# Second block of a two-block model: in-projections in the order head, unit, side work in a fixed 128-point period, and an out projection split in two

## The reference

```python
proj = jnp.einsum('btd,dc->btc', h, w_in[l].astype(jnp.float32))
rw = _token_shift(proj[..., :RWKV_COLS], shift_mu[l])
hg = proj[..., RWKV_COLS:]
...
o_rwkv, v_first = _rwkv7_branch(rw, v_first, ...)
o_hgrn = _hgrn2_branch(hg, lower_bounds[l], g_norm_w[l])
y = jnp.einsum('btc,cd->btd', jnp.concatenate([o_rwkv, o_hgrn], axis=-1), w_out[l])
h = _layer_norm(ALPHA * h + y, ln_w[l], ln_b[l])
```

## Time and profile before

| what | us |
|---|---|
| median of 3 runs | 3117.43 |
| lowest, highest | 3116.45, 3124.18 |
| span of the profiled execution | 3114.6 |
| PE busy | 3019.7 (97%) |
| DVE busy | 1697.0 (54%) |
| ACT busy | 1213.4 (39%) |
| POOL busy | 283.4 (9%) |

### The profile page before, as it was taken

How to read it: one execution, slowest core, us unless ns; L and a number is a source line. 1 busy time by engine, 2 the same in 40 slices (tenths; PEclk the granted TensorE clock), 3 DMA queues, 4 the chain that set the end, 5 groups by cost and what they waited for, 6 DMA issues and landing times.

```text
span 3114.6 us, 39362 instructions
## 1 busy us (share of the span) xinstructions
PE 3019.7 (97%) x15418; PEld 2423.6 (78%) x15418; DVE 1697.0 (54%) x2880; ACT 1213.4 (39%) x2131; POOL 283.4 (9%) x517
## 2 busy tenths in 40 slices
PE   9999999999999999999999999999999999999897
PEld 7778787878788877777778868787787887868786
DVE  6554545454543336556553364656666666565647
ACT  5443434343433324434343333434444343434422
POOL 0110101010100000000000002202022020212001
PEclk9999999999999999999999999999999999999999
DMA  4222222222243321221233322212222131224334
GB/s 164 82 77 84 78 82 82 82 82 82 82 135 131 106 88 62 68 75 62 68 122 134 122 85 80 83 55 90 75 70 90 61 97 56 89 72 140 135 129 155
DMA packets 86007, 288.99 MB, mean 93 GB/s; under 512 B 12080, under 2 KB 12720, under 8 KB 85568
## 3 DMA queue, kind: packets, MB, share of 16 engines
q1 hardware_dynamic: 69696, 243.66, 23.9%
q0 software_dynamic: 16128, 42.81, 4.5%
HBM read 261.13 MB, written 25.17 MB: 92 GB/s over the span
## 4 chain that ended last, share of the span: by engine, by line
PE 83%; DVE 9%; ACT 4%; issue 2%; DMA 1%; POOL 1%; DVEq 0%; ACTq 0%; SPq 0%; POOLq 0%
PE bank L280 14%; PE bank L282 14%; PE bank L281 14%; PE bank L284 7%; PE bank L286 7%; PE bank L285 7%; PE bank L1370 2%; PE bank L1301 1%; PE bank L1306 1%; DVE mc_split L736 1%; PE bank L337 1%; PE bank L317 1%; ACT mc_split L568 1%; PE bank L472 1%; PE bank L485 1%
## 5 line engine op out<-in xcount | busy, mean ns | idle before, releaser
L280 PE MATMUL bank<-ma_split,mc_split 128*128 128x512 f32 x2304 | 957.1, 415 | 12.7 <-DVE ma_split L890 7.7
L736 DVE TENSOR_TENSOR mc_split<-mc,mc_split 128x1024 fp32r<-128x1024 f32 x434 | 534.9, 1233 | 790.1 <-ACT mc_split L568 789.0
L282 PE MATMUL bank<-ma_split,mc_split 128*128 128x512 f32 x2304 | 905.8, 393 | 0.0
L281 PE MATMUL bank<-ma_split,mc_split 128*128 128x512 f32 x2304 | 902.4, 392 | 0.0
L568 ACT ACTIVATE mc_split<-mc 128x1024 fp32r<-128x1024 f32 x434 | 457.8, 1056 | 658.5 <-PE bank L284 349.6
L280 PEld LDWEIGHTS bank<-ma_split,mc_split 128*128 128x128 f32 x2304 | 436.8, 190 | 121.5 <-issue 49.1
L282 PEld LDWEIGHTS bank<-ma_split,mc_split 128*128 128x128 f32 x2304 | 434.6, 189 | 97.0
L281 PEld LDWEIGHTS bank<-ma_split,mc_split 128*128 128x128 f32 x2304 | 436.9, 190 | 78.7 <-issue 4.4
L284 PE MATMUL bank<-mc_split,ma_split 128*128 128x512 f32 x576 | 230.2, 400 | 5.0 <-DVE mb L1780 3.4
L286 PE MATMUL bank<-mc_split,ma_split 128*128 128x512 f32 x576 | 225.3, 391 | 0.0
L285 PE MATMUL bank<-mc_split,ma_split 128*128 128x512 f32 x576 | 224.7, 390 | 0.0
(11 more groups left out here) (366 smaller groups left out, 3732.6 us busy)
## 6 DMA issues: line engine op xcount, KB each, us to landing
mc<-in_w SPq DMA_DIRECT2D x434, 512.0 KB, 3.5
x<-mc POOLq DMA_DIRECT2D x8, 1024.0 KB, 5.2
y<-mb_split SPq DMA_DIRECT2D x28, 256.0 KB, 2.5
ma_split<-y POOLq DMA_DIRECT2D x28, 256.0 KB, 4.5
mb<-in_xt SPq DMA_DIRECT2D x8, 512.0 KB, 9.5
mc<-in_x POOLq DMA_DIRECT2D x4, 1024.0 KB, 5.7
mc<-x POOLq DMA_DIRECT2D x4, 1024.0 KB, 6.5
mats<-mc POOLq DMA_DIRECT2D x32, 128.0 KB, 2.2
```

What stands on the lines that cost most here:

```text
L280: mm = pe.matmul(banks[j][:], wh[:, c], act_hi[:, kt, :], start=(kt == 0), stop=False)
L281: pe.matmul(banks[j][:], wl[:, c], act_hi[:, kt, :], start=False, stop=False)
L282: last = pe.matmul(banks[j][:], wh[:, c], act_lo[:, kt, :], start=False, stop=(kt == KT - 1))
L736: dve.tensor_tensor(w_low[:, s % NR, :, :], w_raw[:, s % NR, :, :], w_high[:, s % NH, :, :].bitcast(F32), ALU.subtract).then_inc(w_lo, 1)
```

## The change

1. **Order of blocks.** rw0, wa, hg0, then rw i, hg i for i = 1 to 7, and then the out blocks. The weights are laid out in the same order.
2. **Period.** All steps of unit u >= 1 begin at 128u+10 (k<12 at two points a step; k 12 to 15 at 2.5; k 16 on at +82, k 25 on at +106, k 36 on at +134). Unit 0 begins at 7 as before. Head h begins at 128h+67 and takes 4.2 points a step (head 7 takes 4.0).
3. **Out blocks.** `most`: kt 0 to 13 of out block 0, 56 points; DVE adds its banks to the residual (`most_take`). Then out block 1, whose last two kt now wait for unit 7 and head 7; then `rest`: kt 14 and 15 of out block 0, 8 points; then out blocks 2 and 3. SP's, POOL's, ACT's and DVE's loops follow the slots; POOL's order of inverses and y loads is as before. Residual loads for group 2 wait for `rest`.

```diff
-BLOCKS = OUT2 + GROUPS
-SLOT0 = [8 * b if b <= WA else 8 * b - 6 for b in range(BLOCKS)]
+OUT2_REST = OUT2 + 2
+BLOCKS = OUT2 + GROUPS + 1
+def slots(b):
+    return {WA: 2, OUT2: BLOCK_SLOTS - 1, OUT2_REST: 1, BLOCKS - 1: 2 * BLOCK_SLOTS}.get(b, BLOCK_SLOTS)
...
-            KIND = [("rw", 0), ("wa", 0), ("rw", 1)]
-            for i in range(UNITS - 2):
-                KIND += [("hg", i), ("rw", i + 2)]
-            KIND += [("hg", i) for i in (UNITS - 2, UNITS - 1)] + [("out", n) for n in range(GROUPS)]
+            KIND = [("rw", 0), ("wa", 0), ("hg", 0)]
+            for i in range(1, UNITS):
+                KIND += [("rw", i), ("hg", i)]
+            KIND += [("most", 0), ("out", 1), ("rest", 0), ("out", 2), ("out", 3)]
...
                 i = k - CHUNKS
-                late = 0 if u else 5
-                if k < PART_B:
-                    return (128 * u - 54 if u else 7) + 2 * k
+                first = 128 * u + (10 if u else 7)
                 if k < CHUNKS:
-                    return 120 * u + 16 + late + 2 * (k - PART_B)
-                begin = 120 * u + 26 + late
+                    return first + 2 * k
+                begin = first + 2 * CHUNKS + 2
                 if i < 4:
-                    return begin + 2 * i
+                    return begin + 5 * i // 2
                 if i < 13:
-                    return begin + 54 + 5 * (i - 4) // 2
+                    return begin + 56 + 5 * (i - 4) // 2
                 if i < CHUNK_K:
-                    return begin + 77 + 5 * (i - 13) // 2
-                return begin + 105 + 3 * (i - CHUNK_K)
+                    return begin + 80 + 5 * (i - 13) // 2
+                return begin + 108 + 3 * (i - CHUNK_K)
...
-                rate = {UNITS - 2: 23, UNITS - 1: 20}.get(h, 45)
-                return 64 * (BLOCK_OF["hg", h] + 1 - LANE0) + 1 + m * rate // 10
+                rate = 40 if h == UNITS - 1 else 42
+                return point0(BLOCK_OF["hg", h] + 1) + 3 + m * rate // 10
...
                         if b == OUT2:
-                            if kt < KT - 2:
-                                pe.wait_ge(y_in[kt // 2], 64)
-                            else:
-                                pe.wait_ge(y_rw_lo if kt == KT - 2 else y_h_lo, UNITS)
+                            pe.wait_ge(y_in[kt // 2], 64)
+                        if b == OUT2 + 1 and kt >= KT - 2:
+                            pe.wait_ge(y_rw_lo if kt == KT - 2 else y_h_lo, UNITS)
...
+            def most_take(dve, b):
+                for t in range(TT):
+                    dve.wait_ge(x2_ready, t + 1)
+                    dve.wait_ge(gemm_done, done(b, t))
+                    dve.tensor_tensor(xr[0][:, t, :], banks[t][:], xr[0][:, t, :], ALU.add).then_inc(bank_free[t], 1)
```

More of the change, by code:

```diff
@@ L56 @@
 OUT2 = RW0 + 2 * UNITS + 1
-BLOCKS = OUT2 + GROUPS
-SLOT0 = [8 * b if b <= WA else 8 * b - 6 for b in range(BLOCKS)]
-TOTAL_SLOTS = SLOT0[-1] + 2 * BLOCK_SLOTS
+OUT2_REST = OUT2 + 2
+BLOCKS = OUT2 + GROUPS + 1
+def slots(b):
+    return {WA: 2, OUT2: BLOCK_SLOTS - 1, OUT2_REST: 1, BLOCKS - 1: 2 * BLOCK_SLOTS}.get(b, BLOCK_SLOTS)
+SLOT0 = [sum(slots(x) for x in range(b)) for b in range(BLOCKS)]
+TOTAL_SLOTS = sum(slots(b) for b in range(BLOCKS))
 Y_ORDER = [*range(UNITS - 1), *range(UNITS, 2 * UNITS - 1), UNITS - 1, 2 * UNITS - 1]
@@ L261, in swa_steps, with products @@
                 return [k for k in range(18) if swa_step_at(g, k) - 8 * s in points]
-            def products(pe, b, lhs_w, act_hi, act_lo, needs, slot0=None, tiles=range(4)):
-                for kt in range(KT):
-                    s = (SLOT0[b] if slot0 is None else slot0) + kt // 2
+            def products(pe, b, lhs_w, act_hi, act_lo, needs, slot0=None, tiles=range(4), kts=range(KT)):
+                first, end = kts[0], kts[-1]
+                for kt in kts:
+                    s = (SLOT0[b] if slot0 is None else slot0) + (kt - first) // 2
                     if kt % 2 == 0:
@@ L1154, in lane_steps @@
                 for point in points:
-                    rw, hg = AT.get(64 * (b - LANE0) + point, ((), ())) if b >= LANE0 else ((), ())
+                    inside = b >= LANE0 and point < 8 * slots(b)
+                    rw, hg = AT.get(point0(b) + point, ((), ())) if inside else ((), ())
                     yield from (("rw", u, k) for u, k in rw)
@@ L1429, in second_pe @@
                         continue
-                    for point in products(pe, b, kind != "out", h_hi, h_lo, needs):
+                    kts = {"most": range(KT - 2), "rest": range(KT - 2, KT)}.get(kind, range(KT))
+                    for point in products(pe, b, kind in ("rw", "hg"), h_hi, h_lo, needs, kts=kts):
                         if b == RW0 and point % 8 == 3:
@@ L1577, in second_act @@
                         continue
-                    for s in range(BLOCK_SLOTS * (1 + (b == BLOCKS - 1))):
+                    for s in range(slots(b)):
                         for lane, u, k in lane_steps(b, range(8 * s, 8 * s + 4)) if s < BLOCK_SLOTS else ():
@@ L1908, in second_dve @@
                             rw_dve(dve, st, u, k) if lane == "rw" else hg_dve(dve, st, u, k)
-                        if kind == "out" and s == 5:
+                        if kind in ("most", "out") and s == 5:
                             dve.wait_ge(x2_in[n % 2], 32 * (n // 2 + 1))
@@ L1917, in second_dve @@
                         hg_take(dve, st, n, b)
+                    elif kind == "most":
+                        most_take(dve, b)
                     elif b < BLOCKS - 1:
@@ L2038, in second_pool @@
                     if n >= 2:
+                        taken = OUT2_REST if n == 2 else OUT2 + 1
                         for t in range(TT):
-                            pool.wait_ge(bank_free[t], freed(OUT2 + n - 1, t))
+                            pool.wait_ge(bank_free[t], freed(taken + 1, t))
                     pool.dma_start(xr[n % 2], x2_rows[:, :, n * N:(n + 1) * N]).then_inc(x2_in[n % 2], 16)
@@ L2131 @@
     wa = w2[:, lo:hi].reshape(2, 8, P, P).transpose(0, 2, 1, 3).reshape(2, P, 2 * N)
-    parts = [w1, rw[0], wa, rw[1]]
-    for i in range(UNITS - 2):
-        parts += [hg[i], rw[i + 2]]
-    parts += [hg[UNITS - 2], hg[UNITS - 1], blocks(x["w_out_2"][0].reshape(KT, P, D)[Y_ORDER].reshape(D, D))]
-    parts.append(parts[-1][-BLOCK_SLOTS:])
+    parts = [w1, rw[0], wa, hg[0]]
+    for i in range(1, UNITS):
+        parts += [rw[i], hg[i]]
+    last = blocks(x["w_out_2"][0].reshape(KT, P, D)[Y_ORDER].reshape(D, D)).reshape(GROUPS, BLOCK_SLOTS, P, 2 * N)
+    parts += [last[0, :-1], last[1], last[0, -1:], last[2], last[3], last[3]]
     w1 = np.concatenate(parts)
```

20 lines of the change are left out of this document (12 added, 8 removed).

## The result

The changed kernel takes 3178.2 us in the median (3175.2 to 3179.1), the kernel before 3117.0 in the same comparison: ratio 1.0189, 95% interval 1.0176 to 1.0202. It is 1.9% slower. The forecast was 3169, with a range from 3132 to 3200. The profiled executions are 3173.4 and 3114.6 us long, 58.8 apart, where the sum had said 51.

A forecast was written before the change was run, and what follows sets the result against it. PE, busy 97% of the span, was taken as the bound, so only its idle time and clock could change. New losses 126.1 us less old 75 gave +51 on 3114.6: 3166 profiled, 3169 us median, range 3132 to 3200.

The forecast's parts named there:

- unit 0's 7.4: Unit 0 keeps its N wait of 4.3, 0.9 at the block's start and its clock, with small additions: 7.4 us.
- Part 1, the squeezed end goes: Heads 6 and 7 get more points a step; 13.9 us at L1370 and the rest of the old 75 us go.
- Part 2, the collision: New unit's first steps meet old unit's end and a head's steps on DVE: PE waits 7.4 us a unit, most at B.
- The prediction's own sign: In the changed kernel's profile, waits under 2 us at B (step 10) would mean the DVE sum is wrong.
- The take: DVE's `rw_take` starts late by 0.9 and k=32's copy stands behind it: together 1.9 us a unit.
- the shared bank: k=0 and m=17 at one point use one bank, so PE waits 0.7 us; the second place counted in the 7.4.
- Part 2, the clock: Slow PE clock after waits: 2.0 us a unit and 3.0 after the stall, against 20 lost in the old pattern.
- Part 3, POOL's queue: The y loads behind unit 7's inverse leave PE idle 26.1 us at the first matmul of `most`; bounds 24 and 32.
- The rival without a stall: Unit 7's inverse or the loads some 26 us quicker, or the order misread: 3140 us; chance 8%.
- cheap: Rival: each period costs 5.5 us, as one of the first seven costs now: 3115 us, no change; chance 9%.
- faster: Rival: DVE absorbs the steps in the fixed pattern at 3 us a period with its clock: 3095 us; chance 5%.
- worse: Rival: a period's waits reach 15 us, each followed by slow clock, or low clock holds after the stall: 3204 us; chance 11%.

The follow-up runs named there:

- Run 3: Kernel before, with only out block 0 cut in two (most, out 1, rest) and head 7 at 4.0 points a step: 3119.6 us against 3118.8.
- Run 5: Changed kernel with steps 39 to 41 of units 0 to 6 standing 8 points later: 3169.5 us.
- run 2: Changed kernel with steps 36 to 41 of units 0 to 5 28 points later, of unit 6 20 points later: 3143.5 us.
- run 12: run 11 without its second edit, so steps 12 on are back and only steps 29 to 35 stay 7 points later: 3073.2 us, ratio to before 0.9854.
- run 1: Changed kernel with the y loads issued by SP instead of by POOL behind unit 7's inverse: 3155.4 us.
- run 4: Changed kernel with run 2's later end and, on POOL, the first 8 of 14 y tiles loaded ahead of unit 7's inverse: 3120.1 us against 3118.8 before.
- run 11: The 3086.2 us version of runs 6 to 12, with steps 29 to 35 of units 0 to 6 7 instead of 5 points later, steps 12 on 1 later: 3108.8 us.
- runs 6 to 12: From run 4's kernel, unit and head steps moved by a few points: 3112.0, 3104.3, 3118.9, 3090.3, 3086.2, 3108.8 and 3073.2 us in turn.

## Why the prediction was right, and where its steps were not

**The sum came out, through two misses that partly cancel.** It had 110 us of new waits (7 times 10.8 is 75.6, 26.1, 1.0, and unit 0's 7.4 with its clock) against 54.6 of old ones: 55 more. Measured are 48.2 more. It had 17 us of new clock against 20 of old, and one us less for points: 4 less. Measured are 10.9 more. So the waits were about 7 too large, the clock about 15 too small, and the result 8 too low.

**Part 1, the squeezed end goes: right.** The waits at the heads' level products, 13.9 us, are not in the list after. Run 3 adds that the split with a slower head 7 doesn't do it; the turns and distances of the units are needed.

**Part 2, the collision: right in cause, near in size, wrong in place.** 7.4 us a unit were foretold, most at B, 2 at k=39 and 1 at m=21; measured are 4.7 at k=39 and 1.6 at B, 6.3. The size is partly luck. From the start of point 11, at 2559.61, to the end of N's read DVE took 31.4 us, not 28.7, and PE's own way to B, its waits taken out, 24.6 us, not 21.3: both sides were some 3 us short, and the difference came near. On PE's side part of this is slow clock, 0.80 from 2582 to 2594. The prediction's own sign, that with waits at B under 2 us the DVE sum is wrong, misleads: DVE was as late as foretold, but PE had waited for it ahead of B. The step that failed is "most at B". I compared DVE's end with PE's arrival at the last consumer only. But m=20's small update stood in the same queue, behind two thirds of the same work (18.6 of 29.0 us, from start to start), and k=39 needs the bank it frees. Run 5 shows that the place hardly matters (6.1 us of waits instead of 6.3), and run 2 that a coincidence was 3.5 of the 6.3; the rest was there without the old unit's end, which I had not separated. The take was foretold at 1.9 and measured at 2.2 (1.3 and 0.9), the shared bank at 0.7 and 0.8. The second place of the shared bank (0.7 at m=18) I had counted inside the 7.4: with it the collision is 7.0. The 0.8 us for `xt` and k=18 don't appear at all. A period was 10.8 in the sum and is 10.0 to 10.3.

**Part 2, the clock: the term that was mis-sized.** I took 2.0 us a unit, 3.0 for the stall, and 20 for what the old pattern loses. The new one is too small: PE's busy time alone is 26.6 us above run 12's, so at least that much is lost on running matmuls after the change, against 17 in the sum. By period, from one unit's step 0 to the next one's, the five whole ones from 2116.05 to 2850.85 have 136.7 to 137.2 us of busy time for 742 or 743 matmuls, and those of run 12 have 133.8 to 134.1. So a period loses at least some 2.9 us, not 2.0, and these five lose 14.5. Their six waits are 0.7 to 4.7 us long; I had priced only what follows one of 4.3. The other 12 us lie ahead of them and behind them: in two more collisions, unit 0's steps and the out blocks. There the sum had 4.0 for the collisions, 3.0 for the stall, which came to about 1 (run 1), and a share of unit 0's 7.4. Whether the old 20 was right too I can't say from these runs; by the busy time before and in run 12 it was at least 15.7.

**Part 3, POOL's queue: right.** One wait at the first matmul of `most`, ended by a y load into `ma_split`, 21.9 us against 26.1 (bound below: 24). The mis-sized term is the 39.8 us from the last G to the fourth load's arrival. After G's last product ended at 2899.8, the first y load issued 30.0 us later, not 33.7, and PE went on at 2935.59, 35.8 us after G. Of the 3.7 us, 3.0 are in POOL's two waits for the inverse's transfers: 4.18 and 5.38 in rows 9, 2.58 and 3.93 after. Why they were shorter no run shows. The rival without a stall falls. The Trainium skill (DMA: Bandwidth & Descriptors, Rules for kernel authors) says to issue a DMA early and to wait late; runs 1 and 4 bear it out, run 1 with 22.7 us for loads of which the first issues 80 us earlier (2850.1 against 2929.85), run 4 with 23.4 against run 2. By the fit in the Trainium skill (DMA: Bandwidth & Descriptors, Anatomy of one DMA) the four loads would be there 4.4 us after the first issue, an estimate. Here it took 5.7 us until PE went on (2929.85 to 2935.59), nearer to the 6.1 of rows 9 and 10.

**Small parts.** Out block 1's bank wait was 1.3 (1.0 foretold). Not foreseen was the 3.8 us at k=17 of unit 7, of which the order and run 11 show the cause. Rows 7 can't show that a table load needs no drain, as I read them, since the root behind the load waited 2.37 us for DVE. The changed kernel's trace shows it: the load of L1475 starts at 2580.87 and takes 1.28 us, and its ACTIVATE starts at 2582.16, so adding nothing was right. The rivals "cheap" and "faster" fall by the period's 10 us, and so does "worse", which had 15; but their mechanism, DVE taking a fixed pattern in its stride, is real: with the places tuned in runs 6 to 12 a stretch of a period's length has 3.8 us of idle (146.70 less 142.89).

## What to carry to other kernels

A static interleave repeats its mistakes: price one period, by asking for every consumer in it, the small ones too, what stands ahead in the producer's queue, and multiply. Where a wait shows up says little; take the late engine's work away or move it, as a wait that is only dodged (run 5) comes back at the next consumer. And an order of 128 points is worth tuning by single points before it is judged: the change as made lost 1.9%, and with a handful of offsets changed, and POOL's order of y loads, the same order of blocks gains 1.5%. The steps of the kernel before were not tuned in this way, so how much of the 1.5% is owed to the order of blocks isn't shown.
